# A decode step that loads the keys of 5 of its 16 score steps already transposed, from a second copy of the paged cache

## What is computed

```python
def mla_sample(x, cache_ckv, cache_kpe, page_table, ...):
    ...
    past_ckv = cache_ckv[page_table].reshape(B, -1, MLA_KV_LORA)
    past_kpe = cache_kpe[page_table].reshape(B, -1, MLA_ROPE)
    ...
    q_lat = jnp.einsum('bthd,rhd->bthr', q_nope, w_uk)
    s = (jnp.einsum('bthr,bkr->bhtk', q_lat, all_ckv)
         + jnp.einsum('bthd,bkd->bhtk', q_pe, all_kpe)).astype(jnp.float32) * MLA_SCALE
    ...
    p = jax.nn.softmax(s, axis=-1)
    o_lat = jnp.einsum('bhtk,bkr->bthr', p, all_ckv)
```

## Time and profile before

| what | value |
|---|---|
| median of 3 timed runs | 2486.35 us (2484.59 to 2491.87) |
| the profiled execution, its own time | 2487.55 us |
| the profiled execution, its span | 2485.9 us |
| PE busy, share of the span | 2417.2 us, 97% |
| DVE, ACT, POOL busy | 994.1, 786.1, 809.6 us |
| mean granted TensorE clock | 0.993 |
| decode, from the first page turn to the last output matmul of pair 3 | 642.16 to 776.2 us |

### The profile page before, as it was taken

One profiled execution on the slowest core, in us unless ns is written; L12 is line 12 of the kernel. 1 busy time (PEld: TensorE's weight loads), 2 busy tenths in 40 slices (PEclk: granted clock), 3 DMA queues, 4 the chain that ended last, 5 costly groups with the idle time before them and its releaser, 6 DMA issues.

```text
span 2485.9 us, 43881 instructions
## 1 busy us (share of the span) xinstructions
PE 2417.2 (97%) x17572; PEld 2298.5 (92%) x17572; DVE 994.1 (40%) x1899; ACT 786.1 (32%) x1420; POOL 809.6 (33%) x440
## 2 busy tenths in 40 slices
PE   8999999899999999999999999999999999999997
PEld 8999999886567999999999999999999799999997
DVE  5222221696433742221263332126566665323223
ACT  5222222414332532222243222223422444222221
POOL 3333333230222143333314333331344223333331
PEclk9999999999999999999999999999999999999999
DMA  3222222231541132222222222222212422222222
GB/s 124 85 79 82 81 86 73 73 102 53 163 141 43 59 94 80 81 84 80 84 68 84 85 84 79 83 83 73 77 52 60 153 68 77 85 82 78 83 84 77
DMA packets 68648, 209.04 MB, mean 84 GB/s; under 512 B 8380, under 2 KB 21181, under 8 KB 68254
## 3 DMA queue, kind: packets, MB, share of 16 engines
q1 hardware_dynamic: 65438, 196.58, 25.5%
q0 software_dynamic: 3072, 10.49, 1.5%
HBM read 199.22 MB, written 7.82 MB: 83 GB/s over the span
## 4 chain that ended last, share of the span: by engine, by line
PE 88%; DVE 9%; ACT 1%; issue 1%; DMA 0%; DVEq 0%; SPq 0%; ACTq 0%
PE psum L1564 26%; PE psum L1566 25%; PE psum L1565 25%; PE psum L1877 1%; DVE h L1030 1%; PE psum L1940 1%; PE psum L2022 1%; DVE y_ffn L1026 1%; DVE x_lo L1000 1%; DVE work L1021 1%; PE psum L1859 1%; DVE w_lo L1009 1%; PE psum L1612 1%; PE psum L1813 1%; PE psum L1882 1%
## 5 line engine op out<-in xcount | busy, mean ns | idle before, releaser
L892 POOL TENSOR_TENSOR w_lo<-raw,w_hi 128x1024 fp32r<-128x1024 f32 (+2 forms) x315 | 734.6, 2334 | 1419.5 <-ACT w_hi L539 1419.4
L1564 PE MATMUL psum<-x_hi,w_hi 128*128 128x288 f32 x3568 | 1073.4, 301 | 20.2 <-DVE x_lo L1000 18.0
L1566 PE MATMUL psum<-x_hi,w_lo 128*128 128x288 f32 x3568 | 1054.0, 295 | 0.0
L1565 PE MATMUL psum<-x_lo,w_hi 128*128 128x288 f32 x3568 | 1053.1, 295 | 0.0
L1564 PEld LDWEIGHTS psum<-x_hi,w_hi 128*128 128x128 f32 x3568 | 672.0, 188 | 36.4 <-DVE x_lo L1000 27.7
L1565 PEld LDWEIGHTS psum<-x_lo,w_hi 128*128 128x128 f32 x3568 | 672.0, 188 | 3.9
L1566 PEld LDWEIGHTS psum<-x_hi,w_lo 128*128 128x128 f32 x3568 | 671.6, 188 | 0.0
L539 ACT ACTIVATE w_hi<-raw 128x1024 fp32r<-128x1024 f32 (+2 forms) x331 | 341.5, 1033 | 795.8 <-DMA raw<-ffn_in 361.4
L1046 DVE TENSOR_TENSOR work<-psum,r_pre 128x288 f32<-128x288 f32 x352 | 160.0, 456 | 662.9 <-PE psum L1566 662.5
L1564 PE MATMUL psum<-gu_hi,w_hi 128*128 128x288 f32 x1408 | 415.5, 295 | 0.0
L1566 PE MATMUL psum<-gu_hi,w_lo 128*128 128x288 f32 x1408 | 414.7, 295 | 0.0
(11 more groups left out here) (264 smaller groups left out, 1847.1 us busy)
## 6 DMA issues: line engine op xcount, KB each, us to landing
raw<-ffn_in SPq DMA_DIRECT2D x176, 512.0 KB, 3.6
raw<-ffn_out SPq DMA_DIRECT2D x64, 448.0 KB, 3.3
raw<-ffn_out SPq DMA_DIRECT2D x32, 512.0 KB, 3.5
raw<-gla_in SPq DMA_DIRECT2D x25, 512.0 KB, 3.6
cache<-cache SPq DMA_DIRECT2D x64, 160.0 KB, 2.6
cache<-cache_r POOLq DMA_DIRECT2D x64, 160.0 KB, 2.9
raw<-mla_wo SPq DMA_DIRECT2D x8, 512.0 KB, 3.5
raw<-gla_wo SPq DMA_DIRECT2D x8, 512.0 KB, 3.6
```

Source lines behind the costliest of these rows:

```text
L892: pool.tensor_tensor(w_lo[slot][:, 0:w], raw[slot][:, 0:w], w_hi[slot][:, 0:w].bitcast(F32), ALU.subtract).then_inc(s_lo, 1)
L1564: pe.matmul(out, wh, xh, start=start, stop=False)
L1565: pe.matmul(out, wh, xl, start=False, stop=False)
L1566: return pe.matmul(out, wl, xh, start=False, stop=stop)
```

## The change

The host hands over a second and a third copy of the cache: `cache_kt`, where each page has the latent dimension on the partitions (128 partitions by 2 by 128 positions, 128 KB), and `cache_pt`, the rotary part turned the same way (64 by 128, 32 KB). For the ten halves in `LAID`, which are those of steps 0, 1, 5, 9 and 13, SP loads the keys from these copies straight into the key buffers (`load_keys`), and `transpose_pages` and the copies by DVE and ACT are left out. The untransposed pages of these halves are still loaded, since the output needs them. A half has four pages, and each takes one `value_load` and two DMAs, so `load_keys` makes 8 DMAs for a half and 80 in all. SP issues the keys of halves 0 to 3 before all its pages; those of halves 10 and 11 ahead of the pages of pair 2; those of 18 and 19 ahead of the pages of pair 3; those of 26 and 27 behind all pages. From half 4 on it first waits for the scores that last read the buffer.

The key buffers change their order in memory: `c_k` holds 4 pages by 2 latent halves by 128 positions, so a score matmul now reads 4 pieces of 128 numbers instead of 512 in a row, and the copies of the halves that are still turned write 4 such pieces. `c_r` holds the rotary part.

```diff
+LAID = (0, 1, 2, 3, 10, 11, 18, 19, 26, 27)
...
-        c_t = [sb(f"c_t{i}", [P, 5, KEYS // 2], offset=ct_at + i * 10 * KEYS) for i in range(C_TS)]
+        c_k = [sb(f"c_k{i}", [P, 4, KT, PAGE], offset=ct_at + i * 10 * KEYS) for i in range(C_TS)]
+        c_r = [sb(f"c_r{i}", [P, 2, PAGE], offset=ct_at + i * 10 * KEYS + 8 * KEYS) for i in range(C_TS)]
...
+        def load_keys(eng, x):
+
+            b, g = batch_of(x)
+            if x >= C_TS:
+                eng.wait_ge(s_score, 2 * (x // 2 - 1))
+            for odd in range(2):
+                with eng.Fori(0, 2) as i:
+                    page = eng.value_load(table[0:1, bass.ds(PAGES * b + 4 * g + odd + 2 * i, 1)], min_val=0,
+                                          max_val=N_POOL - 1)
+                    eng.dma_start(c_k[x % C_TS][:, odd + 2 * i, :, :], io["cache_kt"][page]).then_inc(s_laid[x % C_TS], 16)
+                    eng.dma_start(c_r[x % C_TS][ROPE * odd:ROPE * odd + ROPE, i, :],
+                                  io["cache_pt"][page]).then_inc(s_laid[x % C_TS], 16)
...
+            if not odd:
+                for x in LAID[0:C_TS]:
+                    load_keys(eng, x)
...
             for bp in range(PAIRS):
+                if bp >= CACHES // 2 and not odd:
+                    for x in LAID[2 * bp:2 * bp + 2]:
+                        load_keys(eng, x)
...
                 load_pages(sp, u0, s_cache, 0)
+                for x in LAID[-2:]:
+                    load_keys(sp, x)
...
                 def pages(x):
+                    if x in LAID:
+                        return
...
-                    dve.tensor_copy(c_t[x % C_TS][:, 0:2, :].rearrange("p a t -> p (a t)"), bank[4]).then_inc(s_ctv, 1)
+                    dve.tensor_copy(c_k[x % C_TS][:, :, 0, :], bank[4].rearrange("p (a t) -> p a t", t=PAGE)).then_inc(s_ctv, 1)
...
+                def transpose_pages(x):
+                    if x in LAID:
+                        return
...
+                    if 2 * step in LAID:
+                        for x in (2 * step, 2 * step + 1):
+                            pe.wait_ge(s_laid[x % C_TS], 128 * sum(i <= x and i % C_TS == x % C_TS for i in LAID))
+                    else:
+                        pe.wait_ge(s_ctv, t)
+                        pe.wait_ge(s_cta, 2 * t)
...
+        "cache_kt": a["cache_ckv"][0].reshape(N_POOL, PAGE, KT, P).transpose(0, 3, 2, 1),
+        "cache_pt": a["cache_kpe"][0].transpose(0, 2, 1),
```

More of the change, by code:

```diff
@@ L247, in hybrid_step @@
         s_cache_p = [[sem(f"s_cache_p{i}_{g}") for g in range(GROUPS)] for i in range(CACHES // 2)]
+        s_laid = [sem(f"s_laid{i}") for i in range(C_TS)]
         s_tr, s_ctv, s_cta, s_score, s_snew = (sem(x) for x in ("s_tr", "s_ctv", "s_cta", "s_score", "s_snew"))
@@ L363, in page_part, with batch_of, turned @@
             return cache[b % CACHES][:, pg, c:c + n]
+        def batch_of(x):
+            return 2 * (x // (2 * GROUPS)) + x % 2, x // 2 % GROUPS
+        def turned(x):
+            return sum(i not in LAID for i in range(x))
+        def load_keys(eng, x):
[9 more added lines that the diff above has]
+                                  io["cache_pt"][page]).then_inc(s_laid[x % C_TS], 16)
         def load_pages(eng, u0, landed, odd):
@@ L741, in pages @@
                 def pages(x):
+                    if x in LAID:
+                        return
                     for j in (1, 2):
-                        act.wait_ge(s_tr, 3 * x + j + 1)
+                        act.wait_ge(s_tr, 3 * turned(x) + j + 1)
                         if x >= C_TS and j == 1:
@@ L746, in pages @@
                         if j == 1:
-                            act.activation(c_t[x % C_TS][:, 2:4, :].rearrange("p a t -> p (a t)"), bank[5],
+                            act.activation(c_k[x % C_TS][:, :, 1, :], bank[5].rearrange("p (a t) -> p a t", t=PAGE),
                                            ACT.Copy).then_inc(s_cta, 1)
                         else:
-                            act.activation(c_t[x % C_TS][:, 4, :], bank[6][:, 0:KEYS // 2], ACT.Copy).then_inc(s_cta, 1)
+                            act.activation(c_r[x % C_TS][:, :, :], bank[6][:, 0:KEYS // 2].rearrange("p (a t) -> p a t", t=PAGE),
+                                           ACT.Copy).then_inc(s_cta, 1)
                 for bp in range(PAIRS):
@@ L1281, in pages @@
                 def pages(x):
-                    dve.wait_ge(s_tr, 3 * x + 1)
+                    if x in LAID:
+                        return
+                    dve.wait_ge(s_tr, 3 * turned(x) + 1)
                     if x >= C_TS:
                         dve.wait_ge(s_score, 2 * (x // 2 - 1))
-                    dve.tensor_copy(c_t[x % C_TS][:, 0:2, :].rearrange("p a t -> p (a t)"), bank[4]).then_inc(s_ctv, 1)
+                    dve.tensor_copy(c_k[x % C_TS][:, :, 0, :], bank[4].rearrange("p (a t) -> p a t", t=PAGE)).then_inc(s_ctv, 1)
                 dve.wait_ge(s_rowt, 1)
@@ L1844, in mla, with pages_landed @@
                 last.then_inc(s_rowt, 1)
[L1846 to L1850, removed]
+                def pages_landed(b, g):
                     pe.wait_ge(s_cache[b % CACHES // 2][g], 32 * SP_PAGES * (b // CACHES + 1))
                     pe.wait_ge(s_cache_p[b % CACHES // 2][g], 32 * (4 - SP_PAGES) * (b // CACHES + 1))
+                def transpose_pages(x):
+                    if x in LAID:
+                        return
+                    b, g = batch_of(x)
+                    t = turned(x)
+                    pages_landed(b, g)
                     for j in range(3):
-                        if x >= 1:
-                            pe.wait_ge(*((s_ctv, x) if j == 0 else (s_cta, 2 * x - 2 + j)))
+                        if t >= 1:
+                            pe.wait_ge(*((s_ctv, t) if j == 0 else (s_cta, 2 * t - 2 + j)))
                         if j < 2:
@@ L1869, in group_scores @@
                     bp, g = step // GROUPS, step % GROUPS
-                    pe.wait_ge(s_ctv, 2 * (step + 1))
-                    pe.wait_ge(s_cta, 4 * (step + 1))
+                    t = turned(2 * step + 2)
+                    if 2 * step in LAID:
[4 more added lines that the diff above has]
+                        pe.wait_ge(s_cta, 2 * t)
                     for j in range(4):
@@ L1876, in group_scores @@
                             if j < KT:
-                                last = pe.matmul(out, q_lat[:, j, b, :],
-                                                 c_t[x % C_TS][:, 2 * j:2 * j + 2, :].rearrange("p a t -> p (a t)"),
+                                last = pe.matmul(out.rearrange("p (a t) -> p a t", t=PAGE), q_lat[:, j, b, :],
+                                                 c_k[x % C_TS][:, :, j, :],
                                                  start=j == 0, stop=False)
@@ L1883, in group_scores @@
                                                  q_pes[:, r, b, :],
-                                                 c_t[x % C_TS][:, 4, :].rearrange("p (i t) -> p i t", t=P),
+                                                 c_r[x % C_TS][:, :, :],
                                                  start=False, stop=r == 1)
@@ L1932, in mla @@
                         if pg % 4 == 0:
+                            for e in range(2):
+                                pages_landed(2 * bp + e, f)
                             if f % 2:
```

## The result

The changed kernel takes 2508.22 us (median of 4 runs, 2507.6 to 2508.74) against 2485.47 us of the kernel before (4 runs, 2484.46 to 2491.87). The ratio is 1.0081, with a 95% interval of 1.0068 to 1.0094: slower by 0.8%, which is some 20 us (the medians differ by 22.7). It was forecast as slower, at 2505.5 us, with a range of 2497.5 to 2513.

The account below looks back on a forecast made before the run. PE bounds the kernel, but SP's queue would bound decode from 667 to 771: waits of 31.4 less 14.0 won give 17.4, plus 1.9 for the clock, 19.3 us slower; forecast 2505.5 us, range 2497.5 to 2513.

Parts of the forecast that it names:

- What bounds the kernel: Whole kernel and decode: PE is the path, busy 97% of the span, with SP's queue next in line.
- the gain of 14.0 us: PE in decode: turns removed ahead of steps 0, 4, 8 and 12 save 5.76 + 3 x 2.74 = 14.0 us.
- SP's time for a round: SP's queue: a key round takes 2.18 us, from 1.53 + 0.48 + 0.17, bounded by 2.01 and 3.06.
- The plain DMA at 0.48: SP's key round: the added second DMA costs 0.48 us, like DMAs without a page number.
- the seventh of a page round for the register operation: SP's key round: the added register operation costs (1.53 - 0.36) / 7 = 0.17 us.
- Halves 0 to 3 are a true gain: Ahead of decode: SP ends these keys at 608.6 and catches up on pages, so 5.76 us are won.
- The chain on SP, 667 to 771: Decode: SP issues keys and pages without rest, 41.9 us a pair; step 13 starts 17.4 us late.
- The three waits: PE ahead of steps 5, 9 and 13: waits for keys of 8.4, 11.5 and 11.5 us, 31.4 summed.
- The clock: PE behind each wait: a slow stretch; the first two cost nothing, the one behind step 13 costs 1.9 us.
- Layout: Key buffers: copies in the new order cost nothing; matmuls reading pieces, if dearer, are hidden by PE's waits up to step 13.
- The sum: Whole kernel: 17.4 + 1.9 = 19.3 us slower, with nothing behind decode absorbing it.

Follow-up runs that it names:

- one DMA less: Changed kernel without loading the rotary part from half 10 on, so one DMA per key round; median 2489.5 us, ratio 1.0001 to the kernel before.
- fewer bytes: Changed kernel with all its DMAs, but latent key DMAs carry 32 of 128 partitions from half 10 on; median 2507.98 us, ratio 1.0072.
- 80 turns: Changed kernel with 80 identity-matrix turns on PE ahead of the key waits of steps 5, 9 and 13; 2512.0 us in one execution.
- fixed pages: Changed kernel with constant page numbers for loaded keys instead of table reads, and the loop written out; median 2484.92 us, ratio 0.9974.

## Why the prediction was right

**What bounds the kernel, and the gain of 14.0 us**: right. On three queues decode ends 12.7 us earlier; on one queue, with the six halves that SP has time for, 8.4 of 8.5.

**SP's time for a round**: right in its kind, a little small. A round is 2.24 us, where 2.18 was worked out. The plain DMA at 0.48 was close (the second DMA of a round takes 0.51 to 0.57), and the seventh of a page round for the register operation, 0.17, fits what is left: 2.24 - 1.53 is 0.71 for both, where 0.65 was put. The run with one DMA less makes it 2.24 - 1.48 = 0.76.

**Halves 0 to 3 are a true gain**: right. The keys ended at 610.2 and SP's first page went out at 611.89, where 608.6 and about 610 were worked out, since `q_lat` was evicted at 574.5 instead of 573.7 and the first key DMA went out at 575.81. SP had caught up before decode: it waited for places for 8.2 us in all, and its last page of pair 1 is 1.0 us late. PE ahead of step 0 doesn't wait. The run with these four halves alone has step 13 5.4 us earlier, though of this only 3 to 4 us are left at the end.

**The chain on SP, 667 to 771**: right. Step 13 starts at 772.66 for 770.8. The 1.9 us are the last page of pair 1, issued 1.0 later (667.9), the rounds, 1.3, and a landing of 2.16 us instead of 2.5. That SP's queue and not the transfers sets it is shown by the runs with one DMA less and with fewer bytes. With half of the keys on POOL's queue SP's pair was forecast at 33.2 us and is 702.04 - 668.62 = 33.4 us, from the first key DMA of step 5 to that of step 9, and the waits of PE fell from 27.3 us to 7.3.

**The three waits**: mis-sized, 9.1, 8.9 and 9.3 us for 8.4, 11.5 and 11.5. I had said that the slow clock behind steps 5 and 9 costs nothing because PE has time; true, but then these waits are shorter by just that. PE needed 693.95 - 688.76 = 5.2 us for the scores of step 5 instead of 2.7. The sum of the waits was wrong by 4 us and the start of step 13 wasn't, since SP sets it.

**The clock**: 1.5 us on the path for 1.9. The Trainium skill's rule in "TensorE: Matmul & The Clock Gate", Part 4 "PE-mode transpose", that transposes don't count as activity in the same way, does not hold for the float32 turns here: 80 of them kept the clock at 1.00.

**Layout**: right, shown by the run with the order alone.

**The sum**: 19.3 forecast. The output of pair 3 begins 20.8 us later (1.9 more on SP, 0.4 less for the clock), and 0.8 came back behind decode, which no term of mine foresaw: that the spans differ by 20.0 us is closer than the terms deserve. The medians differ by 22.7, with the four executions of before at 2485.47; later batches had it at 2488.8 to 2491.1. This spread of the kernel before was not in my forecast; against the median of 2491.0 the loss is 17 us.

## What to carry to other kernels

A load that frees the busiest engine is paid on the queue that issues it, so count instructions of the queue and not bytes: a round that reads a page number costs 1.5 us here and a second DMA in it another 0.7 to 0.8, and with 64 KB a page instead of 160 it costs the same. Work out the time of the queue for a period, as if it were an engine, and set it against the period of the bound engine; here 42 against 30 us told the result, and spreading the same loads over three queues turned some 20 us lost into 10 won. Where the queue has idle time of its own (before the stage, behind its last load), the same loads are free.

## What the runs showed of the hardware

- The kernel before varies by 10 us from one execution to the next, 2484.4 to 2494.5, and the time goes with the mean granted clock of TensorE (0.995 to 0.990). In two traces whose decode takes the same time, those of the kernel before and of the order-only run, the lower level (1.2 GHz) was granted for about 37 and 46 us. Half of the difference is 4.8 us, and the spans differ by 4.3. Most of it lies behind decode (7 and 14 us), where PE has gaps of 0.7 to 1.4 us. What starts these stretches is not shown. A gain in the stage ahead can be taken back there in part, as in the run with four halves.
- Float32 turns in place of idle time kept the granted clock at 1.00 ahead of steps 5 and 13; ahead of step 9, where 4.26 us of idle time were left behind the turns, the score block was slow (3.25 us for 1.94).
- 512 columns that a float32 matmul reads in four pieces cost it nothing: 105.46 against 105.45 us over 14 steps.
- A DMA issue takes SP's queue 0.34 us when the reading of a page number stands before it, and 0.47 to 0.59 us when another DMA does. Single ones took 1.26 us (80 turns, at 726.17) and 1.31 us (fixed pages, at 735.44).
